# Fused decoder trunk: attention weights and values in plain fp32, units five rows behind, sigmoids one row ahead, transposes first in a step

## The reference

```
z = q k^T / 8 (per head, s < t only)
A[t,s] = sigmoid(z[t,s]) * prod_{s<j<t} (1 - sigmoid(z[t,j]))
out = A v
```

## Time and profile before

| what | us |
|---|---|
| median of 3 runs (1497.23 to 1498.64) | 1498.63 |
| the profiled execution: span | 1494.4 |
| runs' median less this span: what lies around the span | 4.2 |
| before the first scan | 356.0 |
| stage 0, first scan to first reduction | 189.8 |
| stage 1, to the last reduction | 156.3 |
| drain, to the first matmul of phase4 | 19.7 |
| busy PE / DVE / ACT / POOL | 1320.4 / 1077.6 / 737.9 / 738.9 |

### The profile page before, as it was taken

The page is one execution under the profiler, slowest core; times in us unless marked ns, Lnnn a source line. Parts: engine busy times, 40 slices in busy tenths (PEclk is TensorE's granted clock), DMA queues, the critical chain, the costliest instruction groups (busy, mean ns, idle before and its releaser), DMA issues.

```text
span 1494.4 us, 18609 instructions
## 1 busy us (share of the span) xinstructions
PE 1320.4 (88%) x6085; PEld 1070.3 (72%) x6085; DVE 1077.6 (72%) x1574; ACT 737.9 (49%) x1268; POOL 738.9 (49%) x676
## 2 busy tenths in 40 slices
PE   2789999994777888887798889999999999999997
PEld 2656888784565666665587668888888888888886
DVE  4848589998767777765477897666666666477787
ACT  4426577744777777776313743332323333354332
POOL 1153445464445438888100245555555556587552
PEclk9998899997998989999799999999999999999999
DMA  9670134355343323321554325444444446788532
GB/s 336 193 211 18 57 127 140 129 171 153 90 100 71 71 72 113 92 72 36 215 181 139 113 85 184 150 159 157 161 162 161 154 156 225 295 300 318 187 113 113
DMA packets 124395, 223.35 MB, mean 149 GB/s; under 512 B 9450, under 2 KB 52564, under 8 KB 124052
## 3 DMA queue, kind: packets, MB, share of 16 engines
q1 hardware_dynamic: 124308, 222.27, 45.4%
HBM read 160.90 MB, written 57.93 MB: 146 GB/s over the span
## 4 chain that ended last, share of the span: by engine, by line
PE 40%; DVE 7%; issue 2%; DMA 1%; ACT 1%; POOL 0%; DVEq 0%; POOLq 0%; ACTq 0%
PE ps_out L2160 25%; PE ps_out L2186 12%; PE ps_out L1497 2%; PE ps_out L1513 1%; DVE mod_acc_final L1580 1%; DMA scr_mod_final<-mod_acc_final 1%; DVE y_full L1601 1%; DVE wgu_lo L2267 0%; ACT square_junk L2078 0%; DVE x L2422 0%; DVE y_gated L1613 0%; DVE down_part L2420 0%; DVE h_sum_t L2234 0%; DVE h_t_full L2234 0%; DVE x L2444 0%
## 5 line engine op out<-in xcount | busy, mean ns | idle before, releaser
L1857 POOL TENSOR_TENSOR wgu_lo<-wgu_raw,wgu_hi 128x512 fp32r<-128x512 f32 x66 | 97.4, 1484 | 127.9 <-ACT wgu_hi L1849 127.9
L2094 POOL TENSOR_TENSOR dn_lo<-dn_raw,dn_hi 128x512 fp32r<-128x512 f32 x77 | 126.4, 1659 | 67.7 <-ACT dn_hi L2000 67.6
L1849 ACT ACTIVATE wgu_hi<-wgu_sum 128x512 fp32r<-128x512 f32 x88 | 55.2, 632 | 199.3 <-DVE wgu_sum L2250 80.3
L2160 PE MATMUL ps_out<-h_b_t_hi,wgu_hi 128*128 128x512 f32 x352 | 137.4, 390 | 6.7 <-DVE h_b_t_lo L2238 2.6
L2000 ACT ACTIVATE dn_hi<-dn_raw 128x1024 fp32r<-128x1024 f32 x77 | 81.2, 1062 | 114.4 <-PE ps_out L2186 54.7
L2160 PE MATMUL ps_out<-h_b_t_hi,wgu_lo 128*128 128x512 f32 x352 | 137.0, 389 | 0.0
L2160 PE MATMUL ps_out<-h_b_t_lo,wgu_hi 128*128 128x512 f32 x352 | 137.0, 389 | 0.0
L413 POOL TENSOR_TENSOR win_lo<-win_raw,win_hi 128x256 fp32r<-128x256 f32 (+1 forms) x84 | 63.3, 784 | 136.6 <-ACT win_hi L404 136.6
L1150 POOL TENSOR_TENSOR a_rows<-beta,stick_left 128x1024 f32<-128x1024 f32 (+3 forms) x64 | 77.2, 1208 | 107.2 <-DVE stick_left L1198 107.2
L2186 PE MATMUL ps_out<-dn_hi 128*128 128x512 f32 x308 | 120.2, 390 | 0.0
L2186 PE MATMUL ps_out<-dn_hi,dn_lo 128*128 128x512 f32 x308 | 119.8, 389 | 0.0
(11 more groups left out here) (326 smaller groups left out, 3812.3 us busy)
## 6 DMA issues: line engine op xcount, KB each, us to landing
scr_act_sums<-act_sums SPq DMA_DIRECT2D x11, 1792.0 KB, 6.8
dn_raw<-scr_act_sums SPq DMA_DIRECT2D x77, 256.0 KB, 5.2
wgu_raw<-in_w_gate_dram SPq DMA_DIRECT2D x11, 1024.0 KB, 5.4
wgu_raw<-in_w_up_dram SPq DMA_DIRECT2D x11, 1024.0 KB, 5.3
wd_sums<-in_w_down_dram SPq DMA_DIRECT2D x11, 1024.0 KB, 4.9
scr_wd_sums<-wd_sums SPq DMA_DIRECT2D x11, 1024.0 KB, 4.1
dn_raw<-scr_wd_sums SPq DMA_DIRECT2D x44, 256.0 KB, 7.3
win_raw<-in_w_in_dram SPq DMA_DIRECT2D x20, 512.0 KB, 4.5
```

The costliest lines, as they stand in the source:

```text
L1857: pool.tensor_tensor(sl[slot(m, x)][:], src, sh[slot(m, x)][:].bitcast(F32), ALU.subtract).then_inc(wlp, 1)
L2094: pool.tensor_tensor(bl[q % NSLOT][:, 1], braw[entry(q)][:, 1], bh[q % NSLOT][:, 1].bitcast(F32), ALU.subtract).then_inc(dlw, 1)
L2160: last = pe.matmul(bank(m, b), a[s][:, t], h[x][t // 2][:, t % 2], start=(fresh and t == 0 and a is sh and h is hh), stop=(t == 3 and a is ...
```

## The change

- The products of the weights with the values (L1324) take plain fp32 operands: one matmul with `aT` in place of two with `aT_hi` and `aT_lo`. The split on ACT and DVE is gone; one engine copies a unit's transposed weights, ACT or DVE in turn (`by_act`), each with its own semaphore. NA goes from 3 to 6 (the same memory).
- The values tile `sb_v` holds plain fp32 values of a pair of heads, 64 columns each, instead of hi | lo of one head. It is made once per pair: hi and lo rows of the transposed values are loaded as two tiles of 128 partitions (`load_values`), and both are multiplied by a rounded identity and added in PSUM, which transposes and joins them. `vd` holds the same fp32 values twice. Both halves of `ps_o` are full results, of which the half of the head's own partitions is copied to `o_full`; `o_lo_part` is gone.
- `load_head` has six DMAs.
- ACT takes the sigmoids of row r+1 in step r.
- PE's order in a step: value transposes, unit transposes, logits of row r+2, products. Where a transpose's place is the slot of the coming logits it now waits itself for the scan (or reduction) of row r-1 (`await_place`).
- LEAD goes from 4 to 5.

```diff
-    NZ, LEAD, VSTEP = 3, 4, 3
+    NZ, LEAD, VSTEP = 3, 5, 3
+    def values_at(r):
+
+        return r < SBR and r % (2 * NT) == VSTEP
-    NB, NPB, NA = 3, 2, 3
+    NB, NPB, NA = 3, 2, 6
-    ah, al = at("aT_hi", [P, NA, HALF], 24, F32R), at("aT_lo", [P, NA, HALF], 30, F32R)
-    tmp = at("o_lo_part", [HD, HALF], 36)
+    aT = at("aT", [P, NA, HALF], 24)
+    def by_act(n):
+
+        gr, b = units[n]
+        return b % 2 == (0 if upper(gr) or gr < SBG else 1)
+
+    def copied(n):
+
+        return cpa if by_act(n) else cpd, sum(by_act(m) == by_act(n) for m in range(n + 1))
...
+    def load_values(sp, pair):
+        for x in range(2):
+            row = (2 * (8 + pair) + x) * P
+            sp.dma_start(vt[x][:].bitcast(F32), scr2[row:row + P, :]).then_inc(v_loaded, 16)
     def sync(sp):
         sp.wait_ge(p1.proj, p1.NALL)
+        load_values(sp, 0)
         load_head(sp, 1)
         for h in range(2, NH):
             sp.wait_ge(z_rdy, NT * (h - 1))
-            sp.wait_ge(v_tr, 2 * (h - 1))
             load_head(sp, h)
+            if h % 2 == 0:
+                sp.wait_ge(v_tr, h)
+                load_values(sp, h // 2)
...
     def scalar(act):
+        betas(0)
         for r in range(STEPS):
-            if r < SBR:
+            if r + 1 < SBR:
+                betas(r + 1)
...
             for n in of_step[r]:
+                if not by_act(n):
+                    continue
                 s = slice(left(n), HALF)
                 act.wait_ge(td, n + 1)
                 if n >= NA:
                     act.wait_ge(vd, n - NA + 1)
-                act.activation(ah[:, n % NA, s], place(("u", n))[:, s], ACT.Copy).then_inc(ahr, 1)
-            for gr in ended(r, 1):
-                act.wait_ge(vd, done_by[gr])
-                if gr >= 1:
-                    act.wait_ge(od, gr)
-                act.activation(tmp[:], o[HD:P], ACT.Copy).then_inc(tm, 1)
+                act.activation(aT[:, n % NA, s], place(("u", n))[:, s], ACT.Copy).then_inc(cpa, 1)
...
     def vector(dve):
             for n in of_step[r]:
+                if by_act(n):
+                    continue
-                dve.wait_ge(ahr, n + 1)
-                dve.tensor_tensor(al[:, n % NA, s], place(("u", n))[:, s], ah[:, n % NA, s].bitcast(F32),
-                                  ALU.subtract).then_inc(alr, 1)
+                dve.wait_ge(td, n + 1)
+                if n >= NA:
+                    dve.wait_ge(vd, n - NA + 1)
+                dve.tensor_copy(aT[:, n % NA, s], place(("u", n))[:, s]).then_inc(cpd, 1)
...
-                dve.wait_ge(tm, gr + 1)
+                dve.wait_ge(vd, done_by[gr])
-                dve.tensor_tensor(of[lanes, G], o[0:HD], tmp[:], ALU.add).then_inc(od, 1)
+                dve.tensor_copy(of[lanes, G], o[lanes]).then_inc(od, 1)
...
     def tensor(pe):
+        def await_place(r, e):
+            await_freed(follows[e])
+            if r + NZ - 1 < NR and bank[e] == ("z", (r + NZ - 1) % NZ) and r >= 1:
+                if r - 1 < SBR:
+                    pe.wait_ge(scd, r)
+                else:
+                    pe.wait_ge(tt, r - SBR)
         for r in range(STEPS):
-            if r + NZ - 1 < NR:
-                logits(r + NZ - 1)
-                        last = pe.transpose(place(("v", 2 * h + x))[:, P * b:P * b + P],
-                                            vt[h % 2][:, P * (4 * x + b):P * (4 * x + b) + P], g.ident[:])
+                        for part in vt:
+                            last = pe.matmul(place(("v", 2 * y + x))[:, P * b:P * b + P],
+                                             part[:, P * (4 * x + b):P * (4 * x + b) + P], g.identr[:],
+                                             start=(part is vt[0]), stop=(part is vt[1]))
...
+            if r + NZ - 1 < NR:
+                logits(r + NZ - 1)
-                for part in (ah, al):
-                    last = pe.matmul(o[:, s], v, part[:, n % NA, s], start=(b == 0 and part is ah),
-                                     stop=(b == 4 * upper(gr) + 3 and part is al), skip_group_check=True)
-                last.then_inc(vd, 1)
+                pe.matmul(o[:, s], v, aT[:, n % NA, s], start=(b == 0), stop=(b == 4 * upper(gr) + 3),
+                          skip_group_check=True).then_inc(vd, 1)
```

More of the change, by code:

```diff
@@ L888, in attention @@
 def attention(nc, k, g, A, scr, p1, base):
-    NZ, LEAD, VSTEP = 3, 4, 3
+    NZ, LEAD, VSTEP = 3, 5, 3
     SBR, SBG, SBP = NH * NT, 2 * NH, NPAIR
     lag = lambda gr: 5 if upper(gr) else 3
+    def values_at(r):
+        return r < SBR and r % (2 * NT) == VSTEP
     def extra(r, end):
-        v = [("v", 2 * (r // NT) + x) for x in range(2)] if r < SBR and r % NT == VSTEP else []
+        v = [("v", 2 * (r // (2 * NT)) + x) for x in range(2)] if values_at(r) else []
         return v, [("s", gr) for gr in range(SBG, 2 * SBG) if end.get(gr, -99) + lag(gr) == r]
@@ L911, in attention @@
     bt = at("beta", [P, NB, SEQ], 44)
-    vs = at("sb_v", [P, 2, NT, P], 56, F32R)
+    vs = at("sb_v", [P, 2, NT, P], 56)
     qh, ql, ks = ([at(f"{name}{j}", [P, SEQ], 64 + 16 * j + 4 * x, F32R) for j in range(2)]
                   for x, name in enumerate(("sb_q_hi2", "sb_q_lo2", "sb_k_stack")))
-    vt = [at(f"sb_vT_stack{j}", [P, SEQ], 76 + 16 * j) for j in range(2)]
+    vt = [at(f"sb_vT_{x}", [P, SEQ], 76 + 16 * j, F32R) for j, x in enumerate(("hi", "lo"))]
     pb = at("stick_left", [P, NPB, SEQ + 1], 96)
@@ L1253, in await_freed @@
             else:
[L1254 removed]
+                pe.wait_ge(*copied(n))
         def logits(r):
```

83 lines of the change are left out of this document (43 added, 40 removed).

## The result

Median of 4 runs 1479.13 us (1475.04 to 1479.95), against 1498.64 (1497.23 to 1501.22) of the kernel before on the same chip: ratio 0.986, 95% interval 0.984 to 0.987. The forecast was 1455. The direction and the range held, the size did not; the time is that of the second rival.

A forecast was written before the change was run, and what follows sets the result against it. It took a ring of waits in the stick-breaking heads, not a sum of work, as the bound. Terms of -34.0 there, -0.8 first head, -7.3 sparse heads and -1.5 drain made -43.6, forecasting 1455 us, range 1433 to 1484.

The forecast's parts named there:

- the second rival: Chance 0.19: stick-breaking heads stay at 21.5 us each and the sparse stage gains nothing, total 1479 us.
- The ring: Stick-breaking heads: scan, logits, transposes, hi copy and sigmoids wait on each other, next scan 3.7 us after the scan starting it.
- part 5: Order: sigmoids ahead and transposes first clear waits, six aT buffers end 6.6 us of waits, LEAD 5 gives a step more.
- part 1: Values product (L1324) as two-pass fp32: +3.6 us of PE a head, to 16.8 in stick-breaking heads, 16.7 in sparse ones.
- part 3: Half sums go, ACT -1.2 us a head; the o_full wait moves to the last product, growing about 0.5 us per group.
- the sum for B: Eight sparse heads: 17.8 us for four, 18, 19, 22 and 19 for the others, 149 in all, -7.3.
- drain: After the last reduction: half-sum copy and subtraction leave each last unit, a longer product stays, -1.5 us.
- Part 2: Split removed: one copy a unit, half on each engine; ACT gives up 5.8 us, takes back 2.9; DVE copy 0.65.
- Part 4: Values transposed per pair by 64 float32r matmuls at 0.06 us instead of transposes at 0.11: 3 us less PE in all.
- Half the gain: Chance 0.19: PSUM-place wait, o_full wait and POOL's paired work limit gains to -18 stick-breaking, -2 sparse: 1479 us.
- PE's clock: Chance 0.05: in the stick-breaking heads PE partly drops to 1.2 GHz, 26.9 us a head, total 1518.
- The slack stays on top: Chance 0.06: surplus over the longest engine persists, 22.9 us a stick-breaking head and 21.3 a sparse one, total 1504.

The follow-up runs named there:

- e10: Kernel before the change with only the sigmoids issued one row ahead: median 1480.1 us, ratio 0.986.
- e4: Changed kernel with each row's sigmoids put back in its own step, the rest kept: median 1484.1 us, ratio 0.989.
- e7: Changed kernel with POOL's modulation products and additions cut to 32 of 512 columns for all blocks but the first: median 1459.1 us, ratio 0.972.
- e1: Changed kernel with the values product as two float32r matmuls of operands rounded once, instead of one fp32 matmul: median 1453.7 us, ratio 0.968.
- e8: Changed kernel with the stick-breaking heads' finished outputs (o_full) copied by ACT instead of DVE: median 1472.4 us, ratio 0.981.
- e17: Changed kernel with the modulation on DVE as a fused instruction and stick-breaking outputs copied by ACT: median 1462.8 us, ratio 0.976.
- e18: Changed kernel with modulation on DVE, stick-breaking outputs copied by ACT, and the values product as two once-rounded float32r matmuls: median 1436.3 us, ratio 0.958.
- e2: Changed kernel with LEAD set back from 5 to 4: median 1484.1 us, ratio 0.988.
- e5: Changed kernel's fp32 precision part alone, with the old order (LEAD 4, logits first, sigmoids in their own step): median 1500.3 us, ratio 1.000.
- e3: Changed kernel with logits ahead of the transposes again in PE's step: median 1479.4 us, ratio 0.985.

## Why the prediction was wrong, point by point

- **The ring: right as the bound of before, wrong as to what was needed.** "The ring, not a sum of work, sets A" holds: e10 opens it alone and gives 17.7 us in A, some 7 of them by the clock. One reading of the turn was off: the scan at 455.77 is not "the next" and waits for nothing; a scan of 896 columns stands between (453.38). The logits of 452.11 belong to the 640-column scan at 458.24, 6.2 us after the end of the scan that let them start. But once the fp32 product fills PE, sigmoids ahead hardly matter (e4). Of part 5, LEAD 5 was worth 6.4 in A, transposes first nothing in sum.
- **Failed step, part 1, "PE goes in A to 16.8 us a head, in B to 16.7".** It is 18.2 to 18.5 and about 18 (e7: 136.9 us in 144.0, or 7.6 heads of 19, by the same count). The pass was right (0.43), the blocks too. Missing were the changes of kind (up to 0.8 a head), the logits' first product (4.7 a head at 0.31, not 0.23: 0.4) and the value transposes (16 per pair of heads at 0.11, not 0.06: 0.4): together up to 1.6. What that costs is less: by e1, 3.6 us of PE are worth 1.8 us of a head in A, so this term is worth about 0.8. A came out at 143.6/7 = 20.5 a head, 1.3 over the forecast's 19.2. (Added up again, the longer engine's steps make 19.7, not 19.9, which changes nothing.)
- **Failed step, part 3, the o_full wait.** Named, at 0.5 us per group, but not a term of the sum: A's 19.2 a head had only the step loads of PE and DVE. e8 measured it at 0.9 a head, 6.3 us. With the 0.8 of part 1 that is 20.9, which covers the miss in A.
- **Failed step, part 5 and the sum for B, "17.8 for four heads and 18, 19, 22 and 19 for the others: -7.3".** The loads of POOL were read right and priced as if its work lay beside the rest. PE's and POOL's longest engine were taken one at a time, where PE, at 18 us, now waits in its queue for POOL's diagonals. e7 puts 15.7 us on POOL, against 11.1 missed in B. The DVE waits that were to go (46.2) did go, and were replaced by waits for transposes (33.5 and 23.0). PE's length is a part of these: the first is 30.7 in e17 and 23.6 in e18.
- **Failed step, drain, "-1.5".** A row more of lag is a row more to drain: +3.9, and 19.9 in e2. LEAD 5 was costed at nothing there.
- **Part 2, right:** the copy was taken at 0.65 and is 0.676. **Part 4, wrong by its whole 3 us:** the float32r matmuls at L1333 are 0.11 apart, as transposes are at the same clock. (In seven of the eight heads the value transposes before ran wholly or in part at the lower clock, 0.21 apart; after, only those of the first pair do. The forecast did not count that either.) My row for 0.06 was the hi and lo product at L1324, with one block of values for both. That this is the reason is not shown: the logits' pairs of 128 columns, each with its own block of q, also start 0.06 apart (before: 452.69 and 452.75, after: 7 of 14 in A). The rule of the Trainium skill (Perfetto Trace Analysis, Transposes), to issue a transpose as one, is neither borne out nor contradicted by equal spacings.
- **First head, a gain missed:** -3.4 where -0.8 stood. The precision part alone costs it 2.7 (e5); LEAD gives 1.7 (e2), the transposes' place 2.9 (e3) and the sigmoids 2.3 (e4). The first scan came 1.9 us earlier, which says nothing: it lies between 353.4 and 358.4 us in all these kernels.
- **The rivals.** "Half the gain" gave the total, and of its three named mechanisms two are shown (o_full, POOL's paired work); its A, 21.5 a head, was too long and its B, -2, too short, so that the right total is partly luck. PE's clock is refuted: 1.00 in A with PE at 92%. The Trainium skill's rule on transposes beside it (TensorE: Matmul & The Clock Gate, Part 4) gave that rival some weight; no fall is to be seen in A, with 36 of them a head. "The slack stays on top" gave 22.9 a head and is refuted too; in B it took ACT (14.9) for the longest engine, where POOL had 124.1/8 = 15.5. Of the signs named, one failed: POOL is busy 77% of B, not over 80.
- **What stays open:** why the same POOL work costs B 3.8 us more under the fp32 product than under the split. With the split PE waited for a diagonal 10 times in B, at most 1.3 us; in e5 2.5. That PE's longer steps shift it against POOL's queue is argued, not shown. And how much of A's gain the clock would give with the order held.

## What to carry to other kernels

Undo each wait in both kernels, with the rest of the change and without it: 26.9 us of waiting for sigmoids was worth 17.7 us before (with the clock that came back), and 24.0 us of it 1.9 once PE was full. When a change makes one engine the longest, count its work by the start-to-start spacing of every kind in the order in which it will run, changes of kind included, and price the missing part by what an experiment says a us of it is worth; 10% of PE's work was some 11 us of work in A here, and about half of that in time. And look at what stands ahead of a small producer in its queue: background work that fills an idle engine is free only until the engine it feeds has no slack.

## What the chip showed unexpectedly

- The float32r matmuls of 128 columns at L1333 start 0.11 us apart, a hi and lo pair of the values product or of the logits 0.06; what decides is not shown.
- The first logits matmul of 512 columns has its partner 0.31 us later behind a transpose in A of the kernel after (33 of 39), and behind an fp32 product in e3. In the kernel before it was mostly 0.23 behind a float32r product and 0.30 or more where PE had stood idle.
- The granted clock was 1.00 in A with PE at 92% of the time by spacing, where it was 0.88 when PE had more gaps. A fall of 6.8 us to 1.2 GHz behind a wait of 2.2 us made the same head 24.8 us long in place of 22.2.
- The fused product and addition on DVE took 0.74 us alone, for what POOL did in 1.04 and 1.28, and up to 1.87 beside a POOL addition on SBUF, which in turn made the next POOL instruction longer.
